# Sums of squares on the four column parts of the array, then copied, added and spread by one product

## The reference

```
def rms_norm(x, g):
    xf = x.astype(jnp.float32)
    y = xf * lax.rsqrt(jnp.mean(xf * xf, axis=-1, keepdims=True) + EPS)
    return y.astype(x.dtype) * g
```

## Time and profile before

| | |
|---|---|
| Median of 3 runs | 2309.62 us (2307.52 to 2311.8) |
| Profiled execution, own time | 2310.19 us |
| Its span in the profile | 2308.1 us |
| TensorE busy | 2141.5 us (93%) |
| VectorE, ScalarE, GpSimd busy | 1552.1 (67%), 1151.8 (50%), 489.6 us (21%) |
| Granted TensorE clock, mean | 0.965 of full speed |

### The profile page before, as it was taken

How to read it: one execution, slowest core, us unless ns; L and a number is a source line. 1 busy time by engine, 2 the same in 40 slices (tenths; PEclk the granted TensorE clock), 3 DMA queues, 4 the chain that set the end, 5 groups by cost and what they waited for, 6 DMA issues and landing times.

```text
span 2308.1 us, 42283 instructions
## 1 busy us (share of the span) xinstructions
PE 2141.5 (93%) x17432; PEld 1970.9 (85%) x17432; DVE 1552.1 (67%) x2301; ACT 1151.8 (50%) x1917; POOL 489.6 (21%) x628
## 2 busy tenths in 40 slices
PE   6999979999999998899998989989998999998998
PEld 3985549999999995589997889989997888998997
DVE  3657766777777756667776769756555677965554
ACT  3534444555655642555556555554444655554443
POOL 0011330333233002213321043202110124311110
PEclk8999999999999998999999999999999999998999
DMA  8535444555465443335553435544553433553552
GB/s 325 164 128 220 165 183 146 178 195 177 155 201 185 153 165 128 147 119 188 187 190 104 157 104 191 173 138 164 185 190 103 146 128 129 165 185 127 191 191 84
DMA packets 103199, 378.21 MB, mean 164 GB/s; under 512 B 11584, under 2 KB 11744, under 8 KB 101984
## 3 DMA queue, kind: packets, MB, share of 16 engines
q1 hardware_dynamic: 101520, 367.31, 46.7%
q10 hardware_dynamic: 1488, 8.20, 0.9%
HBM read 374.42 MB, written 1.05 MB: 163 GB/s over the span
## 4 chain that ended last, share of the span: by engine, by line
PE 35%; issue 8%; DVE 6%; POOL 3%; ACT 3%; POOLq 0%; DVEq 0%; ACTq 0%
PE ps L396 10%; PE ps L397 10%; PE ps L398 10%; DVE WL L1572 2%; PE ps L453 2%; POOL R L2521 1%; POOL R L2479 1%; ACT WH L968 1%; DVE RST L1608 1%; DVE TMP L1582 1%; PE ps L410 1%; DVE R L1582 1%; PE ps L411 1%; PE ps L416 0%; POOL X L2284 0%
## 5 line engine op out<-in xcount | busy, mean ns | idle before, releaser
L396 PE MATMUL ps<-X,WH 128*128 128x256 f32 x4384 | 1243.4, 284 | 13.6 <-DVE WL L1572 12.5
L397 PE MATMUL ps<-X,WH 128*128 128x256 f32 x4384 | 1228.7, 280 | 0.0
L398 PE MATMUL ps<-X,WL 128*128 128x256 f32 x4384 | 1225.8, 280 | 0.0
L1572 DVE TENSOR_TENSOR WL<-RAW,WH 128x1024 fp32r<-128x1024 f32 (+2 forms) x608 | 802.7, 1340 | 461.3 <-ACT WH L968 460.6
L396 PEld LDWEIGHTS ps<-X,WH 128*128 128x128 f32 x4384 | 826.9, 189 | 28.3 <-DVE WL L1572 17.6
L397 PEld LDWEIGHTS ps<-X,WH 128*128 128x128 f32 x4384 | 827.4, 189 | 1.4
L398 PEld LDWEIGHTS ps<-X,WL 128*128 128x128 f32 x4384 | 827.1, 189 | 0.0
L968 ACT ACTIVATE WH<-RAW 128x1024 fp32r<-128x1024 f32 (+2 forms) x608 | 625.7, 1047 | 383.7 <-PE ps L398 362.5
L1106 ACT ACTIVATE PB<-ps,SM 128x512 f32<-128x512 f32 (+1 forms) x152 | 87.7, 584 | 156.4 <-DVE SM L1745 156.2
L2326 POOL TENSOR_SCALAR R<-CONS,SM 128x128 f32<-128x128 f32 x128 | 84.4, 670 | 360.5 <-DVE SM L1755 360.5
L2418 POOL TENSOR_TENSOR TMP<-TMP 128x256 f32<-128x256 f32 x66 | 49.0, 742 | 438.3 <-ACT TMP L1288 434.8
(11 more groups left out here) (184 smaller groups left out, 2157.5 us busy)
## 6 DMA issues: line engine op xcount, KB each, us to landing
RAW<-w_dram SPq DMA_DIRECT2D x674, 512.0 KB, 3.8
RAW<-w_dram SPq DMA_DIRECT2D x16, 480.0 KB, 3.1
BIG<-big_dram ACTq DMA_DIRECT2D x4, 1024.0 KB, 5.1
RAW<-w_dram SPq DMA_DIRECT2D x8, 320.0 KB, 2.7
RAW<-w_dram SPq DMA_DIRECT2D x6, 384.0 KB, 3.0
XT<-x_dram ACTq DMA_DIRECT2D x2, 1024.0 KB, 10.9
CONS<-con_dram ACTq DMA_DIRECT2D x1, 1105.0 KB, 5.0
out_dram<-XT SPq DMA_DIRECT2D x1, 1024.0 KB, 3.9
```

What stands on the lines that cost most here:

```text
L396: e.matmul(out, a.hi, b.hi, start=start and i == 0, stop=False, skip_group_check=open_bank)
L397: e.matmul(out, a.hi, b.lo, start=False, stop=False, skip_group_check=open_bank)
L398: last = e.matmul(out, a.lo, b.hi, start=False, stop=stop and i == n - 1, skip_group_check=open_bank)
L1572: e.tensor_tensor(weights(i).lo, raw(i), weights(i).hi.bitcast(F32), ALU.subtract).then_inc(*w_lo.mark(i))
```

## The change

A sum whose number of chunks is a multiple of four (17 of the 21) is made in three steps. Four squared chunks are multiplied at a time, each by 32 columns of the ones, each on a column part of the array of its own, with its result on 32 partitions of the bank (`flush`). When all groups are in, the bank holds four partial sums, each repeated on 32 partitions. ScalarE copies them to `RST`'s buffer (signal `parted`), TensorE multiplies them by a new constant `four`, which has ones in the rows 0, 32, 64 and 96, into columns 256 to 511 of the bank, and the square root reads those. TensorE's `rstd` waits for `parted` before this product. The sums of two chunks stay as they were (`whole`). The output projection with a hook keeps two chunks waiting instead of four, and the first transfer of constants grows from 257 to 385 columns.

```diff
--- before.py
+++ after.py
@@ -26,7 +26,7 @@
       ("gkc", 1), ("gsub", 1), ("cw", 132), ("cb", 44), ("lam", 128)]
 P2 = [("pre", 8), ("qn", 2), ("kvn", 2), ("scw", 12), ("cfw", 124), ("cfb", 4), ("lng", 4), ("lnb", 4),
       ("gb", 32), ("post", 8), ("fpre", 8), ("fpost", 8)]
-CONSTS = [("ident", 128), ("ones", 128), ("eps", 1), ("sel", 256), ("selT", 512), ("swap", 128), ("swapm", 32),
+CONSTS = [("ident", 128), ("ones", 128), ("eps", 1), ("four", 128), ("sel", 256), ("selT", 512), ("swap", 128), ("swapm", 32),
           ("cosA", 256), ("sinA", 256), ("cosC", 256), ("sinC", 256), ("mask", 256), ("invf", 1), ("sgn", 1)]
 
 
@@ -259,6 +259,8 @@
 
         lin, acc, sums, folded, spread, swapped = (signal(n) for n in ("lin", "acc", "sums", "folded", "spread", "swapped"))
         scored, turned, valued, adaturn, mixed = (signal(n) for n in ("scored", "turned", "valued", "adaturn", "mixed"))
+
+        parted = signal("parted")
 
         w_hi, x_hi, squares, roots, copied = (signal(n) for n in ("w_hi", "x_hi", "squares", "roots", "copied"))
         exps, opened, conv0, gated = (signal(n) for n in ("exps", "opened", "conv0", "gated"))
@@ -443,7 +445,22 @@
                     self.n += 2
 
                 def flush(self, keep=0):
-                    while len(self.pend) > keep:
+                    if self.total % 4:
+                        return self.whole()
+                    while len(self.pend) >= 4 + keep:
+                        for _, place in self.pend[:4]:
+                            q.wait_ge(*squares(self.tag, place))
+                        if self.i == 0:
+                            q.wait_ge(s_con, 16)
+                            wait(self.bank.free)
+                        for x in range(4):
+                            b, _ = self.pend.pop(0)
+                            e.matmul(self.bank.ap[32 * x:32 * x + 32, 0:256], ones[:, 0:32], b.ap, start=self.i == 0,
+                                     stop=self.i == self.total - 4).then_inc(*sums.mark(self.tag, self.i + x))
+                        self.i += 4
+
+                def whole(self):
+                    while self.pend:
                         (b, place), i = self.pend.pop(0), self.i
                         self.i += 1
                         q.wait_ge(*squares(self.tag, place))
@@ -454,6 +471,9 @@
 
                 def rstd(self, out):
                     self.flush()
+                    if self.total % 4 == 0:
+                        q.wait_ge(*parted(self.tag))
+                        e.matmul(self.bank.ap[:, 256:512], con("four"), out.ap, start=True, stop=True).then_inc(*sums.mark(self.tag, "all"))
                     self.bank.free = [roots(self.tag)]
 
             def ada_turn():
@@ -730,7 +750,7 @@
                         bank, _ = tile([X[st][:, c] for c in range(8)], [((x_lo if c > 5 else y_lo)(("att", l, st), c),) for c in (6, 7, 0, 1, 2, 3, 4, 5)],
                                        (6, 7, 0, 1, 2, 3, 4, 5))
                         bank.free = [resid(tag, m)]
-                        ss.flush(keep=1 if between is None else 4)
+                        ss.flush(keep=1 if between is None else 2)
                         ss.add()
                         if between is not None:
                             between(m)
@@ -1021,7 +1041,12 @@
                     q.wait_ge(*sums(self.tag, self.total - 1))
                     q.wait_ge(s_con, 16)
                     wait(out.free)
-                    e.activation(out.ap, self.bank.ap[:, 0:256], ACT.Sqrt, scale=1.0 / size, bias=eps).then_inc(*roots.mark(self.tag))
+                    total = self.bank.ap[:, 0:256]
+                    if self.total % 4 == 0:
+                        e.activation(out.ap, total, ACT.Copy).then_inc(*parted.mark(self.tag))
+                        q.wait_ge(*sums(self.tag, "all"))
+                        total = self.bank.ap[:, 256:512]
+                    e.activation(out.ap, total, ACT.Sqrt, scale=1.0 / size, bias=eps).then_inc(*roots.mark(self.tag))
 
             def ada_step(ring=PS):
                 k.todo.pop(0)
@@ -1158,7 +1183,7 @@
 
 
             e.dma_start(PARS[:, 0:80], par_d[:, 0:80]).then_inc(s_par, 16)
-            e.dma_start(CONS[:, 0:257], con_d[:, 0:257]).then_inc(s_con, 16)
+            e.dma_start(CONS[:, 0:385], con_d[:, 0:385]).then_inc(s_con, 16)
             e.dma_start(XT[:, 0], x_d[:, 0]).then_inc(s_x, 16)
             e.dma_start(PARS[:, 80:npar], par_d[:, 80:npar]).then_inc(s_par2, 16)
             e.dma_start(posb, pos_d).then_inc(s_pos, 16)
@@ -1175,7 +1200,7 @@
                         ss.add(XT[:, 0, n], (s_x, 16))
                     ss.rstd(1024, k.rst[0])
                 if c == 6:
-                    e.dma_start(CONS[:, 257:ncon], con_d[:, 257:ncon]).then_inc(s_con2, 16)
+                    e.dma_start(CONS[:, 385:ncon], con_d[:, 385:ncon]).then_inc(s_con2, 16)
             for _ in modulate(("n1", 0, 0), 0, 0, X[0], lag=8):
                 pass
             e.dma_start(BIG[:], big_d[0]).then_inc(s_big, 16)
@@ -2726,6 +2751,7 @@
     put("ident", np.eye(128))
     put("ones", 1.0)
     put("eps", EPS)
+    put("four", (p % 32 == 0)[:, None])
     sel, selT = np.zeros((128, 4, 2, 32)), np.zeros((128, 4, 128))
     for k in range(128):
         for t in range(4):
```

## The result

The changed kernel takes 2322.55 us (median of 4 runs, 2321.17 to 2327.49) against 2308.57 (2306.24 to 2311.8) for the kernel before beside it: a ratio of 1.0063, interval 1.0044 to 1.0083, some 14 us slower. Its profiled execution took 2322.42 us with a span of 2320.6 and a mean granted clock of 0.958. A later set of runs of the same kernel gave 1.006 (1.0043 to 1.0077).

A forecast was written before the change was run, and what follows sets the result against it. TensorE, busy for 93% of the span, was taken as the bound. Losses of 14.35 us where it goes on, less 3.2 gained where it waits, made 11.1 slower: median 2320.7, 8 in 10 between 2314 and 2327.

The forecast's parts named there:

- First early hook: `out` of stream 1, closed in the first feed-forward after tile pair 4: TensorE stalls for ScalarE's copy, 5.0 us lost.
- Second early hook: `add` of stream 0, closed in the second feed-forward: TensorE stalls until ScalarE arrives for the copy, 4.7 us lost.
- Clock together: Behind the two feed-forward stalls the granted clock falls to half: 2.2 us lost at each, 4.4 in all.
- The tail's price: From last square to square root, group, copy, spreading product and signals take 1.83 us, about 2.9 at half clock.
- `out` of stream 0: Sum closed after stream 1's first tile: six products before it become one group, 1.8 us gained; net 0.7 gained.
- `out` of layer 1: Output projection: five products before the last tile become one group, 1.38 us gained; longer tail, 1.04 lost; net 0.35 gained.
- `add` of stream 1: Closed in layer 1's projection: TensorE would leave 2.4 us later but waits 2.66 for a low half anyway; 0.4 lost.
- the two stalls are made up: Rival, 8%: the engines catch up and the two feed-forward stalls cost nothing; 3.0 us gained, 2307.
- about no change: Rival, 6%: both feed-forward stalls last, the clock does not fall, half of each is recovered; 14.1 becomes 4.9, 2311.5.
- the four column products do not overlap: Rival, 2%: each group of four takes 1.72 us and all gains turn, about 2330.
- The products count: Rival, 4%: the round trip doesn't count and all 17 sums return their queue time, 23 us, 2287.
- The clock costs more: Rival, 10%: sparse products in `fpre` and `pre` leave feed-forwards starting at half clock; stalls' clock reaches 3.0 each; 2326 to 2329.

The follow-up runs named there:

- Run 1: Changed kernel with the two sums closed by the feed-forwards' early hooks made the old way, the other 15 new: 2310.65 us, ratio 1.0008 to the kernel before.
- run 2: Kernel before with only the two early-hook sums made in groups, copied and spread: 2324.63 us, ratio 1.0068 to the kernel before.
- Run 3: Changed kernel with TensorE's wait and spreading product at the two early hooks moved one tile pair later: 2309.97 us, ratio 1.0009 to the kernel before.
- run 8: The changed kernel again, unedited, in a later comparison: 2323.18 us, ratio 1.006 to the kernel before.
- run 4: Changed kernel with 14 unused float32 products issued before each of the two early-hook waits: 2320.34 us, ratio 1.0049 to the kernel before.
- run 7: Changed kernel with the new form only in the two `fpost` sums: 2306.15 us against 2309.26 for the kernel before, ratio 0.9985.
- run 6: Changed kernel without copy and spreading product, the square root reading partial sums (output not the reference's): 2296.52 us, ratio 0.9943 to the kernel before.
- run 5: Changed kernel with full-width sums instead of groups, copy, wait and spreading product kept: 2332.48 us against 2309.26 for the kernel before, ratio 1.0096.

## Why the prediction was right

It said 2320.7, between 2314 and 2327, and slower with 82%; measured were 2322.55. The two runs of the profile lie 12.23 apart (2322.42 and 2310.19), where 11.1 were forecast. The mechanism is the one predicted, at the places predicted. TensorE's queue is in order, so a wait put into it costs as much as the releasing engine is behind at that point. Runs 1 and 2 show that two places carry the whole loss. Run 3 shows that it is the place of the wait and not the round trip: the same instructions behind one more pair of tiles cost 3.0 us by the ledger instead of 12.2, and nothing that the times can tell. The terms, one by one:

- **First early hook**: 5.0 for the stall, 2.2 for the clock and 0.25 back made 6.95; measured 5.63, and 8.23 in run 8. TensorE stood for 6.84 and 6.68, as forecast (7.0). The clock took 1.6 in the one and 3.0 in the other, so the 2.2 lies between.
- **Second early hook**: 4.7 + 2.2 = 6.9; measured 6.58, and 6.71 in run 8, with 6.41 and 6.24 of standstill (forecast 6.6) and 2.6 and 2.8 for the clock.
- **Clock together**: 4.4 forecast. By the windows 4.2 in the first profile and 5.8 in run 8; against run 4, where it stays at 1.00, the stages lost 3.8 and 6.6 more.
- **The same two in one sum**: 6.95 + 6.9 = 13.85 forecast; 12.2 by the ledger, 14.9 in run 8 and 13.2 in run 2.
- **Everything else together** was to gain 2.7 (11.1 less 13.85). Run 1 is that part alone and gives 1.0008: 1.8 us lost, with an interval from 1.6 gained to 5.3 lost. The sign may be wrong, and several terms are. In the profile the two parts err against each other, the hooks by 1.6 less than forecast and the rest by the 2.7 that it didn't gain, so that the total comes closer than its parts, which is luck.
- **The tail's price** is the one that recurs. From the last square to the square root 1.83 us were forecast; 2.07 to 2.09 were measured at both `post` and both `fpost`, 2.21 at `out` of layer 1 and 2.60 at `add` of layer 1. At the end of the kernel the missing quarter lies in the last group: the copy starts 0.90 after the last square, not 0.64 and a signal. For half clock the forecast's 2.9 is added up wrongly: both matmul terms doubled give 1.28 + 0.38 + 1.18 + 0.22 = 3.06, and 3.04 were measured at `fpre` and `pre`. So `fpre` had nothing to gain.
- **`out` of stream 0** is the first place that came out wrong: 0.7 gained was forecast. The position before it (the attention's last reciprocal, 300.51 in the kernel before) had moved by -0.24, the next reciprocal by +0.73: 1.0 lost. The timeline there:

```profile
367.01 0.64 PE L458 MATMUL ps<-PB,CONS 128*32 128x256 f32 x8
367.29 1.22 DVE L1597 TENSOR_TENSOR WL<-RAW,WH 128x1024 fp32r<-128x1024 f32 x1 [1.53 <-ACT WH L988]
...
368.94 0.42 ACT L1026 ACTIVATE PB<-XT 128x256 f32<-128x256 f32 x1 [1.69 <-DVE XT L1607]
369.26 0.37 ACT L1046 ACTIVATE RST<-ps 128x256 f32<-128x256 f32 x1
369.68 1.22 PE L476 MATMUL ps<-RST,CONS 128*128 128x256 f32 x2 [2.03 <-ACT RST L1046]
```

  The prediction let the 1.8 us saved on products move everything forward, ScalarE with it. But TensorE doesn't set ScalarE's pace here. The residual's addition (line 1607) stands in VectorE's queue behind the cutting of a weight tile (line 1597), which waits for ScalarE's high half (1.53). That chain gains little: from one square to the next it took 3.23 and 3.24 us before and 3.06 and 3.14 now. So the copy comes at 369.26, only 0.95 earlier than the square root did, and TensorE waits for it for 2.03. Then the clock falls, too: 0.53 in the 1.4 us behind it and 0.65 in the next 3, where the same stretch of the kernel before had 1.00:

```profile
369.60:371.00 1.40, 1.32 (x4) 1.14 (x5) 0.00 (x0) 0.09 (x2) 0.00 (x0) 0.53 0.71 281
371.00:374.00 3.00, 3.00 (x19) 3.00 (x19) 2.44 (x4) 0.56 (x2) 0.00 (x0) 0.65 0.10 37
```

- **`out` of layer 1** is the second such place: 0.35 gained was forecast, 1.0 lost measured (its reciprocal moves from 15.84 late, in the attention before it, to 16.88). The timeline at its tail has the round trip that was priced:

```profile
1030.24 0.64 PE L458 MATMUL ps<-PB,CONS 128*32 128x256 f32 x8 [2.10 <-ACT PB L1026]
1031.00 0.38 ACT L1046 ACTIVATE RST<-ps 128x256 f32<-128x256 f32 x1 [0.90 <-PE ps L458]
```

  But TensorE stood for 2.10 before the last group: the products saved earlier were not what the last square waited for. From the first square to the last it took 21.40 us instead of 21.78, so 0.38 was received of the 1.38; the tail grew from 0.79 to 2.21, so 1.42 was paid and not 1.04. That the cutting of the weights holds it up here as well follows from the same order of the queues; no run took it apart.
- **`add` of stream 1**: 0.4 lost was forecast. From 781.32 to the next shared wait, at 834.37, the lateness goes from 12.95 to 12.33, so 0.6 was gained. The wait of 2.66 of the earlier trace rows has no counterpart any more: the delay went into slack, as said, and somewhat more came back. TensorE does stand there: 3.10 us for the copy, at 803.43.
- **`add` of layer 1**: 0.2 lost was forecast; with its feed-forward it lost 0.8 (0.1 gained in run 8). Its tail alone grew from 1.65 to 2.60.
- **The tails**: `fpost` of block 0 gained 2.6 (1.5 forecast) and that of block 1 0.95 (1.0), each with the feed-forward before it. The second is partly luck: the tail alone gained 0.78 (2.08 for 2.86), and in run 8 the same stage lost 0.8 with the same tail. The two `post` gained 0.6 and 0.25 (0.35 each). `fpre` was to gain 0.15 in all and lost 0.3 and 0.4; `pre` was to lose 0.3 and lost 0.7. Besides the tail's price, this is what was overlooked at `fpre`:

```profile
1570.11 1.08 PE L458 MATMUL ps<-PB,CONS 128*32 128x256 f32 x8 [6.45 <-ACT PB L1026]
...
1571.24 0.72 ACT L1026 ACTIVATE PB<-XT 128x256 f32<-128x256 f32 x2 [0.18 <-PE ps L458]
```

  The last two squares wait 0.18 for TensorE's first group. There are six buffers for squares, and a full-width product freed one after each square, a group frees four at once and later.
- **What the change doesn't touch** moved by up to 3.6 us either way. The attention of layer 1 lost 3.5 (the lateness goes from 12.33 to 15.84), the stage up to `cf` of block 0 lost 3.3, and the one up to `cf` of block 1 gained 3.6. For the last two the trace has the place. In both blocks 3.2 us lie at the same run of products with 32x32 weights (line 867, line 847 before), and what differs is the clock. Below are the two blocks before, then the two after:

```profile
1279.40:1286.00 6.60, 6.60 (x33) 3.60 (x33) 5.65 (x15) 4.00 (x10) 0.00 (x0) 1.00 0.23 82
...
1825.00:1833.40 8.40, 8.40 (x26) 4.29 (x26) 7.33 (x19) 3.99 (x10) 0.00 (x0) 0.66 0.19 69
```

```profile
1295.60:1304.00 8.40, 8.40 (x26) 4.30 (x25) 7.51 (x19) 3.91 (x10) 0.00 (x0) 0.65 0.17 63
...
1841.50:1848.00 6.50, 6.50 (x33) 3.43 (x32) 5.47 (x14) 4.00 (x10) 0.00 (x0) 1.00 0.23 83
```

  The two cancel here. They needn't: in run 8 block 0 lost 1.5 at this place and block 1 again gained 3.2. The attention of layer 1 lost 3.0 in run 7's profile too, which has no change there. So the last 3 us between the 11.1 forecast and the 14 measured cannot be given to a place.

Of the rivals, *the two stalls are made up* and *about no change* fall with runs 2 and 3, *the four column products do not overlap* with the 0.64 of each group and with run 6. *The products count* falls with run 6: with no round trip at all its sums give TensorE 15 x 1.90 + 2 x 0.95 = 30 us of queue time back, by the forecast's prices, and 13 us arrive. *The clock costs more* gave its standstills 3.0 us each, and run 8 shows 3.0 and 2.8. But that adds 1.4 us to the forecast's 4.4 and doesn't make 2326; the rest was to come from the feed-forwards behind `fpre` and `pre`. TensorE starts that behind `fpre` of block 0 at 0.50 in both kernels, and in the next 4 us the clock is 0.77 instead of 0.89, half a microsecond. The medians are 2322.55 and 2323.18.

The granted clock over the whole profile (0.958 for 0.965) suggests a larger loss than there is, because it counts the time in which TensorE stands. Summed over stretches of 2 us, TensorE's busy time times the missing share of the clock is 66.5 us in the changed kernel and 62.6 before, so 3.9 more, and 63.1 in run 6.

Behind the Trainium skill's sentence that a change of tiling mode drains TensorE ("TensorEngine Tiling (Array Packing)", Key Properties) stands the same row of run 3 as above. From the last full-width product before the group to the next but one after it, 1.00 us pass where steps of 0.116 would give 0.23, so the group takes 0.77 of the queue. Its stream is 0.43, since two groups in a row last 1.07 and one lasts 0.64. A full-width float32 product at such a place takes 0.44 (from 349.61 to 350.28 in the kernel before, less 0.23), so it is not the change of number format that costs. The trace agrees, and puts the mode's share at about 0.34.

## What to carry to other kernels

A result fetched from another engine costs its own latency only where somebody waits for it; in an in-order queue it costs, besides, how far that engine is behind. So ask at each place that calls the helper who is ahead there, and set the wait behind work that doesn't need the result: one tile pair was enough. A busy engine isn't always the one that sets the pace: with no round trip, 30 us of products were removed and 13 came back, nearly all where the next product waits for the sum, and nothing at the two early hooks, where the kernel before keeps TensorE busy all the time. Use the cheaper form place by place; here two sums of 17 gave a version faster than both.

## What the runs showed of the hardware that was not expected

The same untouched products ran at either level of the clock. The four windows on line 867 above show it: 33 records in 6.5 us at 1.00, 26 in 8.4 us at 0.65. It isn't all chance. In block 1 that place was 3.2 us faster than before in every profile of a kernel with the round trip at 15 or 17 sums (the changed kernel twice, runs 1, 3, 4 and 5), 1.6 faster in run 6, and within 0.4 of before in runs 2 and 7. In block 0 it was 1.5 to 3.2 slower in six of the nine profiles and as before in three (runs 1, 2 and 6). What decides the level at this place stays open. The kernel before lay between 2301.43 and 2314.67 over 23 runs, and such shifts fit that spread. So the difference of one stage between two profiles is worth little by itself, even when the stage hasn't been touched.

A short standstill gave both: behind the 2.03 us at the close of `out` of stream 0 the clock was 0.53, and behind the 1.97 at the same place in the other profile of the same kernel (run 8), with TensorE as busy before it, it stayed at full speed:

```profile
370.50:372.00 1.50, 1.37 (x10) 1.32 (x11) 0.13 (x1) 0.55 (x2) 0.00 (x0) 1.00 0.88 300
```
